# Attention in units twice as wide, and the compressed branch of all heads as one batch

## What is computed

```python
s_c = einsum('bghqd,bgnd->bghqn', qb, kc) * scale - m * dist_c      # n = 15 compressed keys
p_c = masked_softmax(s_c, cmp_end[None, :] <= tq[:, None])
o = gb[..., 0:1] * o_c + gb[..., 1:2] * o_s + gb[..., 2:3] * o_w
```

## Time and profile before

| | |
|---|---|
| median of 3 runs | 3539.57 us (3538.93 to 3540.74) |
| the profiled execution | 3540.8 us, its span (first to last instruction) 3539.1 us |
| TensorE matmuls busy | 3312.8 us (94%), mean granted clock 0.934 |
| VectorE busy | 2256.0 us (64%) |
| ScalarE busy | 1500.7 us (42%) |
| attention of layer 0 | 296.2 to 368.1 us |
| attention of layer 1 | 943.1 to 1111.4 us |

### The profile page before, as it was taken

How to read it: one execution, slowest core, us unless ns; L and a number is a source line. 1 busy time by engine, 2 the same in 40 slices (tenths; PEclk the granted TensorE clock), 3 DMA queues, 4 the chain that set the end, 5 groups by cost and what they waited for, 6 DMA issues and landing times.

```text
span 3539.1 us, 57565 instructions
## 1 busy us (share of the span) xinstructions
PE 3312.8 (94%) x21170; PEld 2998.4 (85%) x21170; DVE 2256.0 (64%) x4080; ACT 1500.7 (42%) x2569; POOL 316.5 (9%) x201
## 2 busy tenths in 40 slices
PE   8989899999999998987999999999958999999998
PEld 8976799899656997876999998888748999998887
DVE  7644476386252654565897996555366978985555
ACT  5523354255232432232444444554244444445554
POOL 5500253164000000000000000000010000000000
PEclk9996899799857999998999999999979999999999
DMA  8731376576201453312554445555404544445554
GB/s 328 271 128 72 132 274 229 176 278 250 99 1 48 152 181 107 131 48 84 174 183 143 137 142 172 193 192 194 168 24 152 182 166 143 141 138 193 192 193 139
DMA packets 124692, 561.97 MB, mean 159 GB/s; under 512 B 13840, under 2 KB 14992, under 8 KB 97680
## 3 DMA queue, kind: packets, MB, share of 16 engines
q1 hardware_dynamic: 109728, 506.51, 41.7%
q0 software_dynamic: 14256, 51.91, 3.9%
q10 hardware_dynamic: 576, 1.78, 0.1%
HBM read 559.10 MB, written 1.05 MB: 158 GB/s over the span
## 4 chain that ended last, share of the span: by engine, by line
PE 91%; DVE 6%; ACT 2%; DMA 1%; issue 0%; POOL 0%; DVEq 0%; ACTq 0%; POOLq 0%
PE turn L305 52%; PE gather L305 38%; PE turn L672 1%; ACT arena L1048 1%; DVE arena L1850 1%; DVE arena L1489 0%; DMA arena<-ada_in 0%; DVE arena L1860 0%; DVE arena L1794 0%; DVE arena L1504 0%; DVE arena L1484 0%; DVE ring_low L1540 0%; DVE arena L1745 0%; ACT L1048 0%; DVE arena L1499 0%
## 5 line engine op out<-in xcount | busy, mean ns | idle before, releaser
L1048 ACT ACTIVATE dense<-ring 128x1024 fp32r<-128x1024 f32 x544 | 575.4, 1058 | 377.9 <-PE gather L305 344.3
L1876 DVE TENSOR_TENSOR ring_low<-ring,dense 128x1024 fp32r<-128x1024 f32 x544 | 662.1, 1219 | 69.0 <-ACT dense L1048 66.9
L305 PE MATMUL turn<-expert_src_high,dense 128*128 128x256 f32 x2304 | 668.0, 290 | 33.4 <-DVE ring_low L1876 33.4
L305 PE MATMUL turn<-expert_src_low,dense 128*128 128x256 f32 x2304 | 655.2, 284 | 0.0
L305 PE MATMUL turn<-expert_src_high,ring_low 128*128 128x256 f32 x2304 | 655.0, 284 | 0.0
L305 PE MATMUL gather<-dense 128*128 128x512 f32 x2048 | 633.5, 390 | 4.5 <-DVE dense L2009 4.5
L305 PE MATMUL turn<-rounded 128*128 128x256 f32 x2816 | 517.7, 286 | 39.4 <-DVE rounded L1533 25.3
L1540 DVE TENSOR_TENSOR ring_low<-ring,rounded 128x1024 fp32r<-128x1024 f32 x264 | 402.7, 1536 | 222.4 <-ACT rounded L1048 222.4
L305 PEld LDWEIGHTS turn<-rounded 128*128 128x128 f32 x2816 | 446.6, 195 | 40.8 <-DVE ring_low L1540 36.1
L305 PEld LDWEIGHTS turn<-expert_src_high,dense 128*128 128x128 f32 x2304 | 445.3, 193 | 34.6 <-DVE ring_low L1876 22.8
L305 PEld LDWEIGHTS gather<-dense 128*128 128x128 f32 x2048 | 386.0, 188 | 85.2 <-issue 4.9
(11 more groups left out here) (179 smaller groups left out, 4302.7 us busy)
## 6 DMA issues: line engine op xcount, KB each, us to landing
ring<-tiles_in SPq DMA_DIRECT2D x544, 512.0 KB, 3.3
ring<-stream SPq DMA_DIRECT2D x207, 1024.0 KB, 5.0
arena<-ada_in POOLq DMA_DIRECT2D x96, 512.0 KB, 6.2
arena<-keys_in SPq DMA_DIRECT2D x2, 1024.0 KB, 6.9
arena<-c_in POOLq DMA_DIRECT2D x3, 512.0 KB, 5.2
xT<-x_in SPq DMA_DIRECT2D x1, 1024.0 KB, 4.8
out<-hT SPq DMA_DIRECT2D x8, 128.0 KB, 2.0
arena<-attn_in ACTq DMA_DIRECT2D x1, 784.0 KB, 17.3
```

The lines of the kernel that those rows point to most:

```text
L305: return nc.tensor.matmul(out, lhsT, rhs, start=start, stop=stop, skip_group_check=True)
L1048: return nc.scalar.activation(out, in_, func, **kw)
L1876: V.tensor_tensor(tile_words(t, ring_low).bitcast(R32), tile_words(t), tile_high[:, t % AHEAD, :], ALU.subtract).then_inc(S("tile_low"), 1)
```

## The change

- A unit has two rows of w keys each, side by side in one bank. In MLA the rows are the two heads of a pair (12 units for 24), in the memory part the two token tiles of a head (4 for 8), in layer 1 the selected and the window branch of a head and token tile (24 for 48). In layer 1 the scores of both rows are one matmul with keys of both branches side by side (`shared_k`); otherwise they are two matmuls with different stationary operands.
- VectorE adds the bias and takes the two maxima in one instruction each over 2w columns, and takes one reciprocal of two sums; ScalarE's exp and VectorE's scaling stay one per row. The transposes and the copy behind them cover 2w columns. `biased` has two buffers for three.
- The 24 compressed units are gone. One batch does their softmax: 12 score matmuls (a pair of heads each, keys laid out block-diagonally in `kcmp`, 32 columns) behind the scores of unit 1; on VectorE the bias, the maxima and the subtraction over all 360 columns behind the maximum of unit 1; one exp on ScalarE; sums, reciprocals, gates and scaling on VectorE behind the scaling of unit 1; six transposes on TensorE in loop step 4; two copies on ScalarE. The value product of a head is then one matmul over 32 rows and 256 columns (`compressed_sum`) behind the value matmuls of its second token tile.
- In the compression the hidden values get a tile of their own, padded with zeros to 128 columns and with each group's 15 blocks four times over, so that `vcmp` holds a copy for each row group of 32. Two small ScalarE copies become three, and TensorE waits for six `shared_s` where it waited for five.
- The host's table of distances for the compressed branch is laid out per head, with the slope applied: 360 columns for 30.

```diff
-        kcmp = a.take(GROUPS, N_CMP)
+        kcmp = a.take(GROUPS, 2 * CMP_PITCH)
-        biased = a.take(3, T)
-        probs = a.take(4, T)
-        probs_c = a.take(4, P)
-        probsT = a.take(3, T)
+        biased = a.take(2, 2 * T)
+        probs = a.take(4, 2 * T)
+        probsT = a.take(3, 4 * P)
+        cmp_s = a.take(TT, HEADS * N_CMP)
+        cmp_stat = a.take(3, TT * HEADS)
+        probs_c = a.take(TT, HEADS * 2 * CMP_PITCH)
+        probs_cT = a.take(HEADS // 4, T)
...
+                g, half = i // HPG, HD * (i % 2)
+                keys = shared_k[half:half + HD, :, g, 0:w]
+                u.update(pair=i // 2, halves=[half, half], slope=-alibi_slopes(HEADS)[i],
+                         scores=[(qh[half:half + HD, i // 2, cols], keys)],
...
         def units(m):
+            heads = [("mla", i) for i in range(HEADS // 2)] if m == 0 else [("nsa", h) for h in range(HEADS)]
+            return [unit(kind, i, tt) for kind, i in heads for tt in range(TT)]                + [unit("mem", h, None) for h in range(MEM_HEADS)]
...
             def attend(m):                                      # TensorE
+                def compressed_scores():
+                    for tt in range(TT):
+                        for p in range(HEADS // 2):
+                            at = (tt * HEADS + 2 * p) * CMP_PITCH
+                            last = mm(Y[3][:, at:at + 2 * CMP_PITCH], qh[:, p, tt * P:(tt + 1) * P],
+                                      kcmp[:, 2 * p // HPG, :], True, True)
+                    last.then_inc(S("cmp_filled"), 1)
+                def compressed_turn():
+                    pe.wait_ge(S("cmp_scaled"), 1)
+                    for tt in range(TT):
+                        for b in range(HEADS // 4):
+                            last = nc.tensor.transpose(Y[2 + tt][:, b * P:(b + 1) * P],
+                                                       probs_c[:, tt, b * P:(b + 1) * P], identity)
+                        last.then_inc(S("cmp_turned"), 1)
+                def compressed_sum(h):
+                    if h == 0:
+                        pe.wait_ge(S("cmpT_ready"), 2)
+                    half, rows = HD * (h % 2), slice(2 * CMP_PITCH * (h % 4), 2 * CMP_PITCH * (h % 4 + 1))
+                    return mm(Y[h // 2 % 4][half:half + HD, 0:T], vcmp[rows, h // HPG, :],
+                              probs_cT[rows, h // 4, :], False, True)
...
-                        mm(B[n % 2][:, 0:u["w"]], u["q"], u["k"], True, True).then_inc(S("scores_filled"), 1)
+                        for r, (q, k) in enumerate(u["scores"]):
+                            dst = B[n % 2][:, r * w:(r + 1) * w] if len(u["scores"]) == 2 else two_rows(B[n % 2], w)
+                            last = mm(dst, q, k, True, True)
+                        last.then_inc(S("scores_filled"), 1)
+                    if m == 1 and n == 1:
+                        compressed_scores()
+                    if m == 1 and n == 4:
+                        compressed_turn()
...
+                        if u["kind"] == "nsa" and u["tt"] == TT - 1:
+                            last = compressed_sum(u["index"])
                         last.then_inc(S("head_done"), 1)
...
             def attend(m):                                      # VectorE
+                def compressed_shift():
+                    dve.wait_ge(S("cmp_filled"), 1)
+                    ...
+                    chain.add(V.tensor_tensor(s, src, bias, ALU.add))
+                    chain.wait()
+                    chain.add(V.tensor_reduce(cmp_stat[:, 0, :], s, AXIS.X, ALU.max))
+                    chain.wait()
+                    V.tensor_tensor(s, s, cmp_stat[:, 0, :].unsqueeze(2).to_broadcast([P, TT * HEADS, N_CMP]),
+                                    ALU.subtract).then_inc(S("cmp_shifted"), 1)
+                def compressed_scale():
+                    dve.wait_ge(S("cmp_exp"), 1)
+                    ...
+                    chain.add(V.tensor_reduce(cmp_stat[:, 1, :], s, AXIS.X, ALU.add))
+                    chain.add(V.reciprocal(cmp_stat[:, 1, :], cmp_stat[:, 1, :]))
+                    ...
...
+                        src = two_rows(B[n % 2], w)
+                        if u["slope"] is not None:
+                            with_bias = two_rows(biased[:, n % 2, :], w)
+                            chain.add(V.scalar_tensor_tensor(with_bias, bias_of(u), u["slope"], src,
+                                                             ALU.mult, ALU.add))
+                    if m == 1 and n == 1:
+                        compressed_shift()
...
+                        for r in range(2):
+                            p = two_rows(probs[:, j % 4, :], u["w"])[:, r, :]
+                            inv = row_inv[:, c + r:c + r + 1]
...
+                    if m == 1 and n == 2:
+                        compressed_scale()
...
-                        last = mm(Y[2][0:N_CMP, g * HD:(g + 1) * HD],
-                                  cmp_hid[:, 1, k, g * N_CMP:(g + 1) * N_CMP],
+                        last = mm(Y[2][:, g * HD:(g + 1) * HD], cmp_hid_v[:, k, g, :],
                                   w[:, 2, k * HD:(k + 1) * HD], k == 0, k == 1)
-            pe.wait_ge(S("shared_s"), 5)
+            pe.wait_ge(S("shared_s"), 6)
```

More of the change, by code:

```diff
@@ L424, in heads_filled, with unit @@
             return S("heads_filled"), n + 1 - (n > 3) - (n > 11)
[L427 to L430, removed]
+        def unit(kind, i, tt):
+            cols = None if tt is None else slice(tt * P, (tt + 1) * P)
+            w = T if tt is None else P * (tt + 1)
+            u = dict(kind=kind, index=i, tt=tt, tts=[tt, tt], w=w, slope=None, gates=None)
             if kind == "mla":
-                w = P * (tt + 1)
-                u.update(w=w, q=qh[0:96, h, cols], k=kh[0:96, h, 0:w], bias=("future", NEG),
-                         v=[vh[:, s, h * HD:(h + 1) * HD] for s in range(tt + 1)])
+                u.update(pair=i, halves=[0, HD], slope=NEG,
+                         scores=[(qh[0:96, 2 * i + r, cols], kh[0:96, 2 * i + r, 0:w]) for r in range(2)],
+                         v=[[vh[:, s, (2 * i + r) * HD:(2 * i + r + 1) * HD] for s in range(tt + 1)]
+                            for r in range(2)])
@@ L435, in unit @@
             elif kind == "mem":
-                r = slice(half, half + HD)
-                u.update(w=T, q=q_mem[r, h // 2, cols], k=k_mem[r, h // 2, :], bias=None,
-                         v=[v_mem[:, s, h * HD:(h + 1) * HD] for s in range(TT)])
-            else:
[L440 to L451, removed]
+                half = HD * (i % 2)
@@ new lines, in unit @@
+                u.update(pair=HEADS // 2 + i // 2, halves=[half, half], tts=[0, 1],
+                         scores=[(q_mem[half:half + HD, i // 2, r * P:(r + 1) * P], k_mem[half:half + HD, i // 2, :])
+                                 for r in range(2)],
+                         v=[[v_mem[:, s, i * HD:(i + 1) * HD] for s in range(TT)]] * 2)
+            else:
+                g, half = i // HPG, HD * (i % 2)
+                keys = shared_k[half:half + HD, :, g, 0:w]
+                u.update(pair=i // 2, halves=[half, half], slope=-alibi_slopes(HEADS)[i],
+                         scores=[(qh[half:half + HD, i // 2, cols], keys)],
+                         gates=[gate_t[:, tt, 3 * i + 1 + r:3 * i + 2 + r] for r in range(2)],
+                         v=[[vsw[:, s, (r * GROUPS + g) * HD:(r * GROUPS + g + 1) * HD] for s in range(tt + 1)]
+                            for r in range(2)])
@@ L452, in unit @@
+            u["closes"] = tt != 0 and (kind == "mla" or i % 2 == 1)
+            u["opens"] = tt != 1 and (kind == "mla" or i % 2 == 0)
             return u
         def units(m):
[L455 to L469, removed]
@@ L656, in attend @@
                         u = us[n]
+                        w = u["w"]
                         if n == 0 or u["kind"] != us[n - 1]["kind"]:
@@ L669, in attend @@
                             pe.wait_ge(S("probsT_ready"), u0 + j - 1)
-                        for s in range(len(u["v"])):
-                            src = probs_of(u, j, P) if u["kind"] == "cmp" else probs[:, j % 4, s * P:(s + 1) * P]
-                            last = nc.tensor.transpose(B[2 + j % 2][:, s * P:(s + 1) * P], src, identity)
+                        blocks = 2 * u["w"] // P
+                        for s in range(blocks):
+                            last = nc.tensor.transpose(B[2 + j % 2][:, s * P:(s + 1) * P],
+                                                       probs[:, j % 4, s * P:(s + 1) * P], identity)
                         last.then_inc(S("probs_turned"), 1)
```

134 lines of the change are left out of this document (85 added, 49 removed).

## The result

The changed kernel took 3433.24 us, the median of four runs (3432.80, 3432.90, 3433.57 and 3469.20), against 3539.25 us for the kernel before, timed beside it: ratio 0.9725, 95% interval 0.9663 to 0.9788. Six later runs of the same program gave 3433.20, 3465.01, 3466.42, 3468.68, 3468.70 and 3469.87. So it has two times, near 3433 (four of ten) and near 3468 (six of ten). The mean granted clock is 0.959 in every run of the shorter kind and 0.948 to 0.950 in those of the longer. Both profiles of this kernel are of the shorter kind.

What follows compares the result with a forecast made beforehand. It took TensorE's time at 1.2 GHz as the bound in both attention stretches. Layer 0 -27.3, layer 1 -43.5 and outside +1.3 gave -69.5 us, so 3470 us from 3539.57; range 3428 to 3500.

Steps and rivals of the forecast that it cites:

- rival 1: Whole kernel: clock rises in layer 1's heads too, two at 8.8 us, ten at 5.0; 3432 us, chance 0.25.
- A head at 1.2 GHz: Layer 1 attention: streams, fixed parts and the added 32-row matmul (1.05) make 8.8 us a head, down from 12.25.
- The fill of layer 1: Start of layer 1's attention: batch work leaves TensorE 8.1 us of steady work in 12.4, so 4.3 us lost.
- Layer 1's clock: Layer 1 attention: low through the heads, up after two memory units; stretch 124.8 us, was 168.3.
- Layer 0's clock: Layer 0 attention: up after two MLA pairs at 1.2 GHz, kept for memory units; stretch 44.6 us, was 71.9.
- An MLA pair at 2.4 GHz: Layer 0 attention: TensorE needs 4.0 to 4.1 us a pair, VectorE's sum of at most 4.2 about tying.
- the overlap I took at 0: MLA value matmuls: halves in different array columns might overlap, saving 0.43 us a unit, 5.2 in all; counted as 0.
- Rival 3: Attention: wide units put engines in series, TensorE waiting at every unit; 140 us on top of 3495, 3635 us, chance 0.04.
- Memory units at 2.4 GHz: Memory part of attention: streams 2.13 and fixed 0.58 make 2.7 us a unit of two token tiles.
- The second stationary operand: Scores of MLA and memory units: a second load costs 0 to 0.29 us, at most 4.6 in all; taken as 0.
- Outside: Outside attention: +1.0 us for the compression's value half and an added ScalarE copy, +0.3 for larger constants; +1.3 in all.
- rival 2: Both layers' attention: clock stays low to the end, -44 us in all; 3495 us, chance 0.27.

Runs made afterwards that it cites:

- the halves of the change, each run alone: Against the kernel before: only the compressed branch batched, units one row wide, 3513.18 us; only the two-row units, compressed units kept in the flow, 3487.15 us.

## Why the prediction came out as it did

The time on record, 3470, is the longer of the kernel's two times (3465 to 3470 in six runs of ten); the median of the first runs, 3433, is rival 1's (3432). That rival came so near by luck: its layer 1 was 7.6 us too short (87 for 94.6), its layer 0 6.5 too long (44.6 for 38.1) and the rest 1.7 too long. Step by step:

- **A head at 1.2 GHz: right.** 8.8 expected, 8.80 measured; the 32-row matmul 1.05 expected, 1.04 measured, and the halves of the change, each run alone, gave 10.16 and 10.88. The fixed parts read from the earlier trace rows are real, and they add up.
- **The fill of layer 1: right in sum, not in its parts.** The turn's transposes were to be out 12.4 us after the start; they were at 919.6, 12.3 after it. The 24 compressed scores took 3.79 us, not 2.8: the clock fell among them, and the 0.12 a record of the earlier trace rows is a price near 2.4 GHz (the clock there was 0.94, from 658.6 to 664.2). Later steps were shorter.
- **Layer 1's clock: the step that failed.** "Down through the heads of layer 1" fits six runs of ten, by their times and mean clocks; in the profiled run it rose after 4.5 heads, and the stretch took 94.6 us, not 124.8. Rival 1 had 87, with the rise after two heads. The argument that it rested on, that 64-row scores keep the clock low, was borne out in part: zeros that double their height took 56 us off the kernel before, and no run of the changed one with them was long. But the copy ahead of the exps, with 64 rows, brought four runs of six to 3415 or less as well, so the height weighs and doesn't decide alone. What I missed is that the heads of the changed kernel sit at an edge, where the same work runs at either clock; one time was then the wrong form of forecast.
- **Layer 0's clock: up sooner.** I had two pairs at 1.2 GHz. It was low for 3.5 us, under one pair. In all layer 0 took 38.1 us, not 44.6.
- **An MLA pair at 2.4 GHz: near by two errors.** 4.0 to 4.1 expected, 4.40 measured. TensorE's own work is 3.41, as the kernels with the copy moved show, and not 4.05: the two heads' value matmuls go to different halves of the columns and run side by side. Eight records of them stream 0.85 us at 2.4 GHz one after another, by 0.21 a block, and took 0.60. That is the overlap I took at 0. The Trainium skill (TensorEngine Tiling (Array Packing), Key Properties) says that different tiles can work in parallel, and these rows agree. In the chain of the kernel after, eight records of an MLA unit, and then of a memory unit, where both rows go to the same half:

```profile
321.00 0.60 PE gather L310 x8
...
328.67 1.02 PE gather L310 x8
```

Against it, the loop over VectorE and ScalarE came to 4.40. I had compared VectorE's sum with TensorE's and called it a tie; what counted was the latency of one unit around the loop of queues, 1.08 + 0.70 + 0.70 + 1.37 + 0.44 and 0.1 of hand-overs, with no engine full. Rival 3, engines in series, is this mechanism. It came only at 2.4 GHz, where it costs 1.0 a pair, not in the form that would have made the kernel slower. (Its sum was also short: eight wide memory units, four in each layer, make 27 us and not 13, so 154 for 140.)
- **Memory units at 2.4 GHz: right.** 2.7 expected; scores 1.06, transposes 0.59 and value matmuls 1.02 make 2.67. The second stationary operand costs nothing.
- **Outside: right in sum.** Between the attentions +1.0 as expected. The value half of the compression, eight records, went from 1.03 to 1.95 us (expected 1.6); behind layer 1 another +1.6 that I had not; ahead of layer 0 it was 3.0 us less, for a reason outside the edit, a clock of 0.95 in the stretch of projections where it had 0.91:

```profile
200.00:293.20 93.20, 76.20 (x360) 62.77 (x360) 34.38 (x50) 17.34 (x31) 0.00 (x0) 0.95 0.32 112
```

The rule of the Trainium skill that rival 1 stood on (TensorE: Matmul & The Clock Gate, "Why this matters for your kernels", a continuously busy TensorE gets the full clock) is not what decides here either. After the change TensorE is busy 40.04 of 40.10 us at 0.50 and 24.80 of 24.80 at 1.00, in one stage with the same work. The outcome agreed with rival 1 in its time, and not by that rule.

How the 106 us of the first median divide: rival 2 of the forecast, with the clock low throughout, gives 44; its prices for layer 1 were borne out, and those of MLA at 1.2 GHz were seen in no steady stretch. Of the other 62, 1.7 lie outside the attentions, and the rest is what the clock gave back in both layers, after the 6 that six MLA pairs wait in their loop.

## What to carry to other kernels

Read the granted clock beside the busy time: a stretch that is full at 1.2 GHz has a second gain in it, and it may hang on how many rows the matmuls span. Where an operand has 64 rows of 128, try padding it with zeros before rewriting the schedule: a few lines gave 56 us here, about half of the 106 of this change's shorter runs. When the clock doubles, count the latency of one unit around the queues, not the sums of the engines, and put a copy that another engine waits for ahead of the new unit's work: that took an MLA pair from 4.40 to 3.41 us. Time a kernel several times before believing a median: this one had two.

## What the runs showed of the hardware

- With columns and order of the matmuls the same, score matmuls over 128 rows instead of 64 (and so no change of height behind them) changed the clock of a stage: low 50 us or more against about 7 in the changed kernel, and through all heads against 13 us in the kernel before.
- The same sequence of matmuls ran 40 us at 1.2 GHz and then at 2.4 GHz in one execution, with TensorE busy throughout. 4.85 us of added full-height matmuls brought the rise forward to 927.8 from 961.6, and it held.
- Value matmuls of 64 columns each that go to the two halves of the columns run side by side when they follow each other: eight records in 0.60 us against 1.02 for the same half.
